# A diagonal state space layer: turning tables made by VectorE during attention and kept in DRAM, output tables on GpSimd, state updates ahead of the skip connection

## The reference

```python
def s5_mixer(u, a_re, a_im, log_dt, b_re, b_im, c_re, c_im, d):
    dt = exp(log_dt); mag = exp(lr * dt)
    ab_re, ab_im = mag * cos(li * dt), mag * sin(li * dt)
    cr = ((ab_re - 1) * lr + ab_im * li) / (lr * lr + li * li)   # ci alike
    bb_re = cr * br - ci * bi;  bb_im = cr * bi + ci * br
    bu = einsum('gpc,bsgc->bsgp', bb, uf)
    x  = associative_scan(x[t] = ab * x[t-1] + bu[t])            # complex
    y  = einsum('gcp,bsgp->bsgc', c_re, xr) - einsum(..., c_im, xi) + d * uf
...
    g_a, g_b = split(gelu(y) @ w_glu);  x = x + g_a * sigmoid(g_b)
```

## Time and profile before

| | us |
|---|---|
| median of 3 runs | 2912.49 (2909.01 to 2916.66) |
| the profiled execution | 2912.28 |
| its span | 2910.6 |
| PE busy | 2572.1 (88%) |
| DVE busy | 1808.0 (62%) |
| POOL busy | 1547.8 (53%) |
| S5 stage: end of the norm (HF) to the first glu product | 2174.5 to 2391.1 |

### The profile page before, as it was taken

One profiled execution on the slowest core, in us unless ns is written; L12 is line 12 of the kernel. 1 busy time (PEld: TensorE's weight loads), 2 busy tenths in 40 slices (PEclk: granted clock), 3 DMA queues, 4 the chain that ended last, 5 costly groups with the idle time before them and its releaser, 6 DMA issues.

```text
span 2910.6 us, 36372 instructions
## 1 busy us (share of the span) xinstructions
PE 2572.1 (88%) x12686; PEld 2015.6 (69%) x12686; DVE 1808.0 (62%) x2136; ACT 921.0 (32%) x1315; POOL 1547.8 (53%) x1258
## 2 busy tenths in 40 slices
PE   4888898969999997999598999999955669999998
PEld 3755677747777776777385478888844558888887
DVE  6668855657768766665656476662258963666314
ACT  2023266723444423766212322221112221222102
POOL 4720344535444552554563056677768617766775
PEclk8977799979999997999797799999977889999999
DMA  8846478842333222886421023332520003333222
GB/s 302 267 126 224 168 255 303 306 138 81 94 94 100 77 97 100 318 315 240 142 84 47 0 58 101 96 92 91 134 65 1 1 1 87 101 88 99 94 94 80
DMA packets 316240, 375.70 MB, mean 129 GB/s; under 512 B 51258, under 2 KB 258894, under 8 KB 316022
## 3 DMA queue, kind: packets, MB, share of 16 engines
q1 hardware_dynamic: 258832, 326.14, 34.1%
q10 hardware_dynamic: 34150, 26.77, 3.0%
q0 software_dynamic: 23168, 21.59, 2.3%
HBM read 392.11 MB, written 49.90 MB: 152 GB/s over the span
## 4 chain that ended last, share of the span: by engine, by line
PE 26%; issue 23%; POOL 22%; DVE 13%; DMA 12%; ACT 3%; SPq 1%; POOLq 0%; ACTq 0%; DVEq 0%
POOL WL L790 15%; POOL WH L786 6%; DMA RAW<-in_moe_w 5%; PE PAIR L501 5%; PE PAIR L502 5%; PE PAIR L503 5%; PE BANK L2210 2%; PE PAIR L1788 2%; DVE WL L1884 2%; DMA RAW<-in_ffn_w_up 1%; DVE ADA_SUM L606 1%; ACT WH L1708 1%; DVE ADA_SUM L604 1%; PE BANK L501 1%; PE BANK L502 1%
## 5 line engine op out<-in xcount | busy, mean ns | idle before, releaser
L790 POOL TENSOR_TENSOR WL<-RAW,WH 128x512 fp32r<-128x512 f32 x584 | 813.4, 1423 | 12.2
L501 PE MATMUL PAIR<-HH,WH 128*128 128x512 f32 x1792 | 711.0, 397 | 38.7 <-POOL HL L1080 29.0
L502 PE MATMUL PAIR<-HL,WH 128*128 128x512 f32 x1792 | 701.4, 391 | 0.0
L503 PE MATMUL PAIR<-HH,WL 128*128 128x512 f32 x1792 | 701.1, 391 | 0.0
L785 POOL TENSOR_TENSOR TURN<-ONES 128x1 f32<-128x1 f32 x146 | 36.3, 249 | 931.9 <-PE PAIR L503 853.9
L501 PEld LDWEIGHTS PAIR<-HH,WH 128*128 128x128 f32 x1792 | 339.0, 189 | 121.2 <-issue 40.8
L502 PEld LDWEIGHTS PAIR<-HL,WH 128*128 128x128 f32 x1792 | 339.3, 189 | 71.2 <-issue 2.4
L503 PEld LDWEIGHTS PAIR<-HH,WL 128*128 128x128 f32 x1792 | 338.8, 189 | 71.6
L786 POOL TENSOR_SCALAR WH<-RAW 128x2048 fp32r<-128x2048 f32 x146 | 282.0, 1932 | 0.0
L1884 DVE TENSOR_TENSOR WL<-RAW,WH 128x2048 fp32r<-128x2048 f32 x78 | 178.8, 2294 | 156.9 <-ACT WH L1708 148.4
L1952 POOL DMA_INDIRECT XG<-htok_scratch,GATHER_I x78 | 147.9, 1896 | 212.8 <-PE PAIR L1758 135.2
(11 more groups left out here) (511 smaller groups left out, 4698.0 us busy)
## 6 DMA issues: line engine op xcount, KB each, us to landing
RAW<-in_moe_w SPq DMA_DIRECT2D x156, 512.0 KB
RAW<-in_ffn_w_up SPq DMA_DIRECT2D x88, 512.0 KB
W2RAW<-in_moe_w SPq DMA_DIRECT2D x78, 512.0 KB
ADA_B<-in_ada_w SPq DMA_DIRECT2D x30, 1024.0 KB, 5.3
RAW<-in_ssm_w_in SPq DMA_DIRECT2D x48, 512.0 KB
...
```

Of the source, the lines that this page charges most:

```text
L501: nc.tensor.matmul(o, wh, xh, start=start, stop=False)
L502: nc.tensor.matmul(o, wh, xl, start=False, stop=False)
L503: return nc.tensor.matmul(o, wl, xh, start=False, stop=stop)
L790: ins = pool.tensor_tensor(WL[:, s, c], RAW[:, s, c], WH[:, s, c].bitcast(F32), ALU.subtract)
```

## The change

1. **Turning tables.** Their six instructions for a tile leave GpSimd. VectorE makes them in layer three's attention (`dve_s5_turning`): those of tile h - 1 after `normalise(h)` for h from 1 to 7, those of tile 7 after the last head. SyncE writes each pair of tables to DRAM (`sp_s5_save`, 512 KB each) and reads it into `TURNING` in the S5 stage, when state k - 2 is out (`sp_s5_tables`).
2. **Parameter tables.** For that they are made earlier: the first vectors while the experts' results of layer two come back (`act_s5_exp`, `dve_s5_angles`, `act_s5_vectors`), the rest, the powers, BB and the angles in the input projection (`dve_evin`). ScalarE does the Sin between two copies there and writes BB and TAB to DRAM (`act_s5_spill`); VectorE waits for both writes before the attention; SyncE reads TAB back after the attention layer's first half is out, and BB before the glu units. The loads of B move to the input projection too.
3. **C tables.** TensorE's 16 transposes of `CRAW` move from the start of the stage into PLE (`pe_s5_rows`), ScalarE's copies of them after its gates (`act_s5_rows_end`).
4. **Output tables.** `CAX` is made by GpSimd, in `pool_s5_step`, in eight instructions (with a negated power table `A_NEG`, so that both parts subtract); the products W1X go to a buffer of their own (`W1_PR`), with fewer links between them. The decays have a buffer and a semaphore of their own.
5. **Order of VectorE in step k:** rest of k - 2, states of k, skip of k - 1.
6. **glu units 0 and 1** are split by GpSimd after its S5 tables, not before them.
7. In `dve_evin` the gated MLP's norm goes ahead of `dve_final_x`.

```diff
     def sp_load_all(engine):
...
+        for i in range(2):
+            load_unit(sp, *block_unit(w, i * 256))
+        sp_s5_reload(engine)
+        for i in range(2, 4):
+            load_unit(sp, *block_unit(w, i * 256))
+        sp_s5_save(engine)
         ffn(0)
         ple(0)
         w = t["od_w_glu_2"][0]
+        sp_s5_tables(engine, 0, 2)
         for i in range(KD):
+            if i == 2:
+                sp_s5_tables(engine, 2, KD)
             load_unit(sp, *paired_unit(w, i * P, w, D + i * P))
...
+    def sp_s5_save(engine):
+        for k in range(KD):
+            par = k % 2
+            engine.wait(w["turning"], 2)
+            sp.dma_start(turn_dram[k], TURN_NEW[:, par].rearrange("p a t n -> p (a t n)")).then_inc(turn_saved[par], 16)
...
+    def dve_s5_turning(dve, k):
+        if k >= 2:
+            dve.e.wait_ge(turn_saved[par], 16 * (k // 2))
+        for i, (a, b, c, d, op) in enumerate(((1, 1, 0, 0, ALU.subtract), (0, 1, 1, 0, ALU.add))):
+            dve.e.tensor_tensor(table(i), high(a), low(b), ALU.mult)
+            dve.link(dve.e.tensor_tensor(tmp, high(c), low(d), ALU.mult))
+            dve.e.tensor_tensor(table(i), table(i), tmp, op).then_inc(w["turning"], 1)
+            dve.wait(w["turning"])
...
+    def act_s5_spill(act):
+        act.wait(w["bb"])
+        act.e.dma_start(bb_dram, BB_NEW[:].rearrange("p a t c -> p (a t c)")).then_inc(w["spilled"], 16)
+        act.wait(w["angles"])
+        act.e.activation(TAB_NEW[:], TAB_NEW[:], ACT.Sin, scale=BELOW_TWO_PI).then_inc(w["tab"], 1)
...
     def dve_s5(dve):
-        dve_s5_start(dve)
         def step(e, k):
-            if e is not None or k < KD - 1:
-                dve_s5_prepare(dve, e, k + 1)
+            if e is not None or k > 1:
+                dve_s5_rest(dve, e, k - 2)
+            dve_s5_states(dve, e, k)
             if e is not None or k:
                 dve_s5_skip(dve, e, k - 1)
-            dve_s5_states(dve, e, k)
-            if e is not None or k:
-                dve_s5_rest(dve, e, k - 1)
...
-        split_units(pool.e, plan.u["norm5"] + 2, plan.u["glu"] + 2)
+        split_units(pool.e, plan.u["norm5"] + 2, plan.u["glu"])
         pool_s5(pool)
-        split_units(pool.e, plan.u["glu"] + 2, plan.unit)
+        split_units(pool.e, plan.u["glu"], plan.unit)
```

More of the change, by code:

```diff
@@ L114, in make_plan @@
     moe(1)
+    plan.step("s5a", banks=1)
     norm(4)
@@ L666, in paired_unit @@
         return part(w1, c1, 0), part(w2, c2, 1)
+    s5_sems = {s: sem(f"s5_{s}") for s in ("a_landed", "b_landed", "landed", "vec_in", "vec_out", "index", "consts", "bb", "angles",
+                                           "tab", "spilled", "reloaded", "tab_back", "w1x", "turning", "ca", "decays", "bu", "state",
+                                           "gelu")}
     def sp_load_all(engine):
@@ L2889, in dve_glu @@
         dve_sum(dve, KD - 1, SQ)
-    s5_sems = {s: sem(f"s5_{s}") for s in ("a_landed", "landed", "vec_in", "vec_out", "consts", "bb", "angles", "tab", "w1x",
-                                           "ca", "turning", "bu", "state", "gelu")}
+    turn_landed = [sem("s5_turn_landed0"), sem("s5_turn_landed1")]
+    turn_saved = [sem("s5_turn_saved0"), sem("s5_turn_saved1")]
     CR, CI, STEP_HI, STEP_LO, MAG4 = range(5)
@@ L2900, in build, with sp_s5_reload, sp_s5_tables @@
     GRID = 16384.0
+    def sp_s5_reload(engine):
+        w, sp = s5_sems, engine.e
+        engine.wait(w["spilled"], 32)
+        engine.wait(half_ready, 4)
+        sp.dma_start(TAB[:].rearrange("p a t n -> p (a t n)"), tab_dram).then_inc(w["tab_back"], 16)
+    def sp_s5_save(engine):
+        w, sp = s5_sems, engine.e
+        for k in range(KD):
+            par = k % 2
+            engine.wait(w["turning"], 2)
+            sp.dma_start(turn_dram[k], TURN_NEW[:, par].rearrange("p a t n -> p (a t n)")).then_inc(turn_saved[par], 16)
+        for par in range(2):
+            engine.wait(turn_saved[par], 8 * KD)
+    def sp_s5_tables(engine, first, last):
+        w, sp = s5_sems, engine.e
+        if first == 0:
+            sp.dma_start(BB[:].rearrange("p a t c -> p (a t c)"), bb_dram).then_inc(w["reloaded"], 16)
+        for k in range(first, last):
+            par = k % 2
+            if k >= 2:
+                sp.wait_ge(w["state"], k - 1)
+            sp.dma_start(TURNING[:, par].rearrange("p a t n -> p (a t n)"), turn_dram[k]).then_inc(turn_landed[par], 16)
     def act_s5_rows(act):
@@ L3134, in pool_s5_step @@
                 rows = slice(h * HD, h * HD + HD)
[L3135 to L3137 removed]
+                ins = pool.e.tensor_tensor(W1X[rows, par, part, :, :, h, :], W1_PR[rows, 2 * part], W1_PR[rows, 2 * part + 1], op)
         ins.then_inc(w["w1x"], 1)
         pool.wait(w["w1x"])
+        cr, ci = (bcast(CK[:, i, tiles, :], 2, S5_L + 1) for i in range(2))
+        ar, ai, an = (bcast(a[:, :, tiles].rearrange("p j t -> p t j"), 3, S5_C) for a in (A_POW[:, 0], A_POW[:, 1], A_NEG))
+        for i, (a, b) in enumerate(((cr, ar), (ci, ai), (cr, an), (ci, ar))):
+            ins = pool.e.tensor_tensor(PRP[:, i], a, b, ALU.mult)
+        pool.link(ins)
+        if k >= 2:
+            pool.e.wait_ge(bank_ready, s5_y(k - 2) + 1)
+        for part in range(2):
+            for h in range(2):
+                rows = slice(h * HD, h * HD + HD)
+                ins = pool.e.tensor_tensor(CAX[rows, par, part, :, :, h, :], PRP[rows, 2 * part], PRP[rows, 2 * part + 1], ALU.subtract)
+        ins.then_inc(w["ca"], 1)
+        pool.wait(w["ca"])
         if k >= 2:
             pool.e.wait_ge(w["state"], k - 1)
[L3143 to L3154 removed]
+        pool.e.tensor_tensor(S5_DECAY[:, par], bcast(FIRST[:], 1, 4), bcast(S5K[:, MAG4, tiles], 2, S5_N), ALU.mult)\
+            .then_inc(w["decays"], 1)
     def pool_s5(pool):
@@ L3276, in act_s5 @@
             ins.then_inc(bank_free[(b + m) % 4], 1)
-        act.wait(w["angles"])
-        act.e.activation(TAB[:], TAB[:], ACT.Sin, scale=BELOW_TWO_PI).then_inc(w["tab"], 1)
+    def act_s5(act):
+        w = s5_sems
         act.wait(w["consts"])
@@ L3344, in dve_s5_states @@
         dve.wait(w["bu"])
-        dve.wait(w["turning"])
+        dve.wait(turn_landed[par], 16)
         flat = lambda a: a.rearrange("p t n -> p (t n)")
-        cos, sin, decay = (flat(TURNING[:, par, i]) for i in range(3))
+        cos, sin, decay = flat(TURNING[:, par, 0]), flat(TURNING[:, par, 1]), flat(S5_DECAY[:, par])
         q = [flat(PR[:, i]) for i in range(4)]
@@ L3355, in dve_s5_states @@
         dve.link(dve.e.tensor_tensor(q[2], q[2], q[3], ALU.subtract))
+        dve.wait(w["decays"])
         for i in (0, 2):
```

217 lines of the change are left out of this document (128 added, 89 removed).

## The result

| | before | after |
|---|---|---|
| median of 4 runs, us | 2914.57 | 2889.70 |
| lowest and highest | 2909.01, 2916.98 | 2882.87, 2897.58 |
| after / before (95%) | | 0.9915 (0.9889 to 0.9942) |
| profiled run: time, span | 2912.28, 2910.6 | 2897.58, 2895.8 |
| its mean granted clock | 0.926 | 0.927 |

The change gains 0.85%, 25 us, where 52 were forecast; 2861 was too low, and 2889.7 also lies above the range's end, 2886.

What follows compares the result with a forecast made beforehand. VectorE was taken to bound the S5 stage, TensorE most of the rest. From 2912.3 us, 52.3 gained in the S5 stage and 0.6 lost in the attention gave 2860.6, forecast 2861 us; range 2842 to 2886.

Steps and rivals of the forecast that it cites:

- The new step, TensorE: S5 loop: TensorE's circle from state k over output k to the next output takes at most 18.8 us, below VectorE's 19.4.
- The new step, VectorE: S5 loop: without CAX, VectorE needs 19.4 us a step (bounds 12.4 and 20.4) and stays the bound.
- The new step, GpSimd: S5 loop: GpSimd needs 15.1 us a step, 19 with contention (bounds 15 and 22), close behind VectorE.
- The stage's start: S5 stage: HF ready at about 2171.5, first state update at 2182 instead of 2205.7 (bounds 2178 and 2190).
- The stage's end: S5 stage: last update to glu takes 19.0 us plus 2 for glu splits; ends at 2338.8, gaining 52.3 us.
- Parameter tables in the input projection: Input projection: small instructions delay VectorE by about 3 us, hidden by a 6.43 us wait; cost 0, bounds 0 and +10.
- Attention: Layer three's attention: turning tables hidden in VectorE's waits for seven of eight; the eighth, ahead of the last low half, +0.6 us.
- A sign that the forecast had named: Attention: the forecast would be wrong if this stretch were longer than 115 us.
- Moved work shows: Attention and input projection: tables overrun (+7 us) and the input projection waits (+8); 2876 us, chance 0.11.
- full exclusion: S5 loop: GpSimd's work and VectorE's two-SBUF-input work never overlap; step 23.8 us, total 2892 us, chance 0.10.
- Rival 4: S5 loop: TensorE's circle decides at a high clock with mild contention; step 16.5 us, total 2841 us, chance 0.07.

Runs made afterwards that it cites:

- e1: Changed kernel with the skip of tile k - 1 moved inside the state update of tile k, between the scans and the turning back; 2870.92 us, ratio 0.9842.
- e7: Changed kernel with the skip inside the state update and without GpSimd's CAX tables from tile 2 on; steps 2 to 6 took 15.3 to 15.9 us.
- e4: Changed kernel with the turning tables of tile 7 behind the attention's last low half, not ahead of it; 2885.51 us, attention stretch 117.9 us.
- e11: Changed kernel without the turning tables of tiles 2 to 7 in the attention; 2884.66 us, attention stretch 117.3 us.
- after again: The changed kernel unedited, profiled in a later run; 2888.63 us, ratio 0.9917 to the kernel before.
- e8: Changed kernel with skip mid-update, angles behind gated norm, table 7 last, one glu split ahead of GpSimd's tables, decays on ScalarE, X scaled after attention; 2849.26 us, 0.9784.

## Why the prediction was wrong

- **The new step, TensorE: this failed.** "With the skip out of the state update's way" was read as a gain only. The circle was closed at the wrong place: from state k over output k to the next output, without the bank that output k - 1 holds until the skip reads it. That bank is one more link, from the end of update k over skip k - 1, L3308 and U to update k + 1, and the whole update lies in that circle: 22.2 us, not "at most 18.8". Nor was it counted that low half k - 1, too, now waits behind the skip, with ScalarE's gelu between (some 19.5 us by itself, estimated above). Steps of 21.6 on average instead of 19.4 cost 15.5 us over seven: some 13 in the five middle ones, 7 in the last (26.5 us, where the update takes 20.4 beside the glu splits), less 4.5 in the first (14.9 us), which has no skip. e1 removes both links, and e7 shows the sum without them.
- **The new step, VectorE: too high by 2 to 3 us,** and not the bound. Its own work is 16.7 us a step in after (117.2 / 7), where 19.4 was taken: the contended update is 14.9 to 15.3 us (17.4 and 15.5 were averaged), the low half 0.69 (1.5 taken).
- **The new step, GpSimd: right.** 18.5 us (129.6 / 7), 19 taken; with the skip out of the way it is the bound (e1, e7), not VectorE. Only its parts were off: 128x320 takes 0.76 and 1.2 us (0.82 taken), 64x320 1.2 to 1.5 (1.0 taken).
- **The stage's start: right.** Taking off the 26.4 us by which the output projection's first X is late, HF is ready at 2170.4 (2171.5 taken) and the first update starts at 2180.7 (2182 taken); it follows HF by 10.3 us, as forecast. GpSimd waits 9.51 us for the last X of PLE, and has CAX of tile 0 15.3 us after its memsets (14.5 taken), 1.6 us behind HF; TensorE starts with HF and doesn't wait for CAX.
- **The stage's end:** 18.2 us from the last update to glu, 21 taken. 11.3 of the 52.3 are missing in all, from +15.5 - 1.3 - 2.8 = 11.4.
- **Parameter tables in the input projection: this failed too.** "They delay VectorE by about 3 us" was +10 to 11. 14 and 12 us of work were 20.6 and 21.4, since half of it ran beside GpSimd's splits at two to eight times its length; and the waits of the earlier trace rows were counted as cover without adding up what stands between them. The named bound, +10, was right, the value 0 was not. The credit for "the norm goes first" was void: the tables' start stood ahead of both.
- **Attention: half right.** Seven tables are hidden as said, 0.6 us in all (e4, e11). Table 7 was put at +0.6 for the low half's delay; it was 3.3 in the second profile of after (109.5 us from the first scale instruction to the last low half, 106.2 before), and 2.3 more for TensorE's fall to 1.2 GHz in the longer gap. The step that failed is where the sum began: I had added up VectorE's work from the last head's end and left out table 5, ahead of the last `normalise`, where VectorE had waited only 0.97 us (the row of before shown above). Tables 5, 6 and 7 take 12.2 us, and the waits that could hide them were 0.97 + 1.5 + 6.4 = 8.9; without table 7 they would just have done. ScalarE's HH comes as early as before, when table 6 and the low half behind it are through, so what is left of table 7 then lies on the path. A sign that the forecast had named, an attention longer than 115 us, did come.
- **Nothing else shows as late:** the expert stage (FG_WH starts at 1437.1 in after again, 1437.5 before), SyncE's stores, the transposes in PLE (rest 669.0 in both profiles, and its loss is accounted for by the loop).
- **Rivals.** "Moved work shows" was true (16 us, 15 priced) together with a step that is neither the forecast's nor full exclusion's 23.8. Full exclusion is out: the sum of rival 2, 23.8, stands against e1's steps of 18.5, and 22.6, the sum without the decays, against e8's of 17.4. By the rule of the Trainium skill, "SBUF — State Buffer", "Who interferes with whom", they couldn't be so short; the trace agrees with it only for the small instructions (last section). Rival 4's step of 16.5 is near e7's average in size only: e7's step is VectorE's own sum, not TensorE's circle. The forecast plus 11 us in the loop and 16 in the moved work is 2888: two rivals at once, outside a range that was made from one at a time.
